# Stick-breaking attention heads: the logarithms of the key blocks behind summed on VectorE before the ones product

## What is computed

```python
z = einsum('bhqd,bhsd->bhqs', q_blk, kf) / sqrt(d)
past = key_pos[None, :] < q_pos[:, None]
log_not = where(past, log_sigmoid(-z), 0.0)
later = lax.cumsum(log_not, axis=3, reverse=True) - log_not
w = where(past, exp(log_sigmoid(z) + later), 0.0)
out = einsum('bhqs,bhsd->bhqd', w, vf)
```

## Time and profile before

| | |
|---|---|
| median of 3 executions | 2816.78 us (2816.77 to 2818.41) |
| profiled execution: its own time | 2817.07 us |
| its span | 2815.3 us |
| PE busy | 2766.5 us, 98% of the span |
| DVE busy | 1526.3 us, 54% |
| ACT busy | 1112.6 us, 40% |
| stick-breaking heads | about 1942 to 2335 us of the span |

### The profile page before, as it was taken

One profiled execution on the slowest core, in us unless ns is written; L12 is line 12 of the kernel. 1 busy time (PEld: TensorE's weight loads), 2 busy tenths in 40 slices (PEclk: granted clock), 3 DMA queues, 4 the chain that ended last, 5 costly groups with the idle time before them and its releaser, 6 DMA issues. The chain is left out here.

```text
span 2815.3 us, 33368 instructions
## 1 busy us (share of the span) xinstructions
PE 2766.5 (98%) x13174; PEld 2249.6 (80%) x13174; DVE 1526.3 (54%) x1830; ACT 1112.6 (40%) x1470; POOL 337.5 (12%) x409
## 2 busy tenths in 40 slices
PE   6999999999999999999999999899999999999999
PEld 2678888878888887888888888788878788788787
DVE  6867678774555546676743232534444434533643
ACT  7742222234344343343332332435555543432611
POOL 1011100000334223322311000100000000000000
PEclk8999999999999999999999999999999999999999
DMA  9647767654455554455455333232222223222252
GB/s 399 239 177 264 244 248 275 247 202 145 151 169 159 176 180 135 161 169 181 144 176 204 119 112 106 101 124 90 83 75 83 83 77 107 80 90 99 97 182 92
DMA packets 162122, 439.35 MB, mean 156 GB/s; under 512 B 14768, under 2 KB 59824, under 8 KB 151728
## 3 DMA queue, kind: packets, MB, share of 16 engines
q1 hardware_dynamic: 123360, 307.28, 32.1%
q0 software_dynamic: 15792, 92.99, 9.3%
q10 hardware_dynamic: 22816, 36.97, 3.7%
HBM read 398.11 MB, written 39.06 MB: 155 GB/s over the span
## 5 line engine op out<-in xcount | busy, mean ns | idle before, releaser
L1621 DVE TENSOR_TENSOR WL<-RAW,WH 128x1024 fp32r<-128x1024 f32 (+1 forms) x424 | 516.2, 1225 | 760.0 <-ACT WH L998 576.8
L408 PE MATMUL PB<-HH,WH 128*128 128x512 f32 x2048 | 817.5, 399 | 3.9 <-ACT zp L998 1.8
L413 PE MATMUL PB<-HL,WH 128*128 128x512 f32 x2048 | 802.0, 392 | 0.0
L414 PE MATMUL PB<-HH,WL 128*128 128x512 f32 x2048 | 801.5, 391 | 0.0
L998 ACT ACTIVATE WH<-RAW 128x1024 fp32r<-128x1024 f32 (+1 forms) x424 | 432.9, 1038 | 448.1 <-PE PB L521 259.1
L519 PE MATMUL PB<-WH,HH 128*128 128x512 f32 x1248 | 489.9, 393 | 0.8 <-DVE HL L1621 0.8
L521 PE MATMUL PB<-WH,HL 128*128 128x512 f32 x1248 | 486.1, 390 | 0.0
L520 PE MATMUL PB<-WL,HH 128*128 128x512 f32 x1248 | 485.9, 389 | 0.0
L408 PEld LDWEIGHTS PB<-HH,WH 128*128 128x128 f32 x2048 | 385.0, 188 | 92.0 <-issue 8.4
L414 PEld LDWEIGHTS PB<-HH,WL 128*128 128x128 f32 x2048 | 385.2, 188 | 66.7
L413 PEld LDWEIGHTS PB<-HL,WH 128*128 128x128 f32 x2048 | 385.7, 188 | 65.7 <-issue 3.1
(11 more groups left out here) (314 smaller groups left out, 2712.0 us busy)
## 6 DMA issues: line engine op xcount, KB each, us to landing
RAW<-in_w_in_t SPq DMA_DIRECT2D x320, 512.0 KB, 3.7
AU<-in_w_ada POOLq DMA_DIRECT2D x64, 1024.0 KB, 5.4
RAW<-in_w_out_t SPq DMA_DIRECT2D x96, 512.0 KB, 3.5
bcb<-R SPq DMA_DIRECT2D x64, 256.0 KB, 6.2
S<-so ACTq DMA_DIRECT2D x24, 384.0 KB, 2.4
ebc<-R SPq DMA_DIRECT2D x32, 256.0 KB, 6.3
SY<-evb ACTq DMA_DIRECT2D x32, 256.0 KB, 2.6
yin<-SY POOLq DMA_DIRECT2D x32, 256.0 KB, 4.2
```

What stands on the lines that cost most here:

```text
L408: h.matmul(banks[j], lh, m.HH[:, t, :], start=st, stop=False)
L413: h.matmul(banks[j], lh, m.HL[:, t, :], start=False, stop=False)
L414: ins = h.matmul(banks[j], ll, m.HH[:, t, :], start=False, stop=en)
L1621: return h.tensor_tensor(o, a, b, op)
```

## The change

The logarithms behind are first added up on VectorE, so that one product with `ones` serves for all the blocks behind. A new tile `LC` has 640 columns: 384 for key block 0 (the sum over blocks 1 to 3, for the queries of blocks 1, 2, 3), and 256 for block 1 (the sum over blocks 2 and 3). Block 2 has only block 3 behind it, and uses `LN` as it is. `LC` is split like `LN`, into `LCh` on ScalarE and `LCl` on VectorE. Blocks 1 and 3 now lie side by side in the tiles and share a bank of 512 columns, so three banks and 12 products do for a head. `LCh` and `LCl` lie where `COS` and `SIN` are later, so those two loads now wait for the last head.

```diff
-OFF = [0, 512, 896, 1152]
+OFF = [0, 512, 1024, 896]
+LATER = [(0, 512, (0,)), (512, 512, (1, 3)), (1024, 256, (2,))]
...
 # tensor_program, stick
             P.wait_ge(*at("LNl", hd))
+            P.wait_ge(*at("LCh", hd))
+            P.wait_ge(*at("LCl", hd))
             P.wait_ge(*at("exact"))
-            for sb in range(4):
-                b, bank = take(hb, "later", hd, sb)
-                for jb in range(sb, 4):
-                    for part in (m.LNh, m.LNl):
-                        ins = h.matmul(bank[:, (jb - sb) * 128:COLS[sb]], m.exact["triS" if jb == sb else "ones"],
-                                       part[:, OFF[jb]:OFF[jb] + COLS[jb]], start=jb == sb and part is m.LNh,
-                                       stop=jb == 3 and part is m.LNl)
+            for n, (o, w, blocks) in enumerate(LATER):
+                b, bank = take(hb, "later", hd, n)
+                for part in (m.LNh, m.LNl):
+                    h.matmul(bank[:, 0:w], m.exact["triS"], part[:, o:o + w], start=part is m.LNh, stop=False)
+                if n < 2:
+                    beyond = [x[:, (0, 384)[n]:(384, 640)[n]] for x in (m.LCh, m.LCl)]
+                else:
+                    beyond = [x[:, OFF[3]:OFF[3] + 128] for x in (m.LNh, m.LNl)]
+                to = bank[:, 128:COLS[n]]
+                h.matmul(to, m.exact["ones"], beyond[0], start=False, stop=False)
+                h.matmul(to, m.exact["ones"], beyond[1], start=False, stop=True).then_inc(*put(P.side, "later", hd, n))
 # scalar_program, stick
             A.then(act(m.LNh, m.LN, ACT.Copy), "LNh", hd)
             yield
-            yield
-            A.wait_ge(*at("logw", hd, 3))
+            A.wait_ge(*at("LC", hd))
+            A.then(act(m.LCh, m.LC, ACT.Copy), "LCh", hd)
+            yield
+            A.wait_ge(*at("logw", hd, 2))
 # vector_program
+    def later_blocks(hd):
+        LN, LC = m.LN, m.LC
+        V.then(h.tensor_copy(LC[:, 384:512], LN[:, OFF[2]:OFF[2] + 128]))
+        V.then(h.tensor_copy(LC[:, 0:128], LN[:, OFF[1]:OFF[1] + 128]))
+        t = V.then(TT(LC[:, 512:640], LN[:, OFF[2] + 128:OFF[2] + 256], LN[:, OFF[3]:OFF[3] + 128], ALU.add))
+        V.wait_ge(*t)
+        V.then(TT(LC[:, 128:384], LN[:, OFF[1] + 128:OFF[1] + 384], LC[:, 384:640], ALU.add), "LC", hd)
...
             yield
+            V.wait_ge(*at("ln masked", hd))
+            later_blocks(hd)
             V.wait_ge(*at("LNh", hd))
+            V.wait_ge(*at("LC", hd))
             V.then(TT(m.LNl, m.LN, m.LNh.bitcast(F32), ALU.subtract), "LNl", hd)
+            V.wait_ge(*at("LCh", hd))
+            V.then(TT(m.LCl, m.LC, m.LCh.bitcast(F32), ALU.subtract), "LCl", hd)
 # gpsimd_program, ahead of the loads of COS and SIN
+    G.wait_ge(*at("later", 7, 2))
```

More of the change, by code:

```diff
@@ L345, in memory @@
     m.COS, o = mem("COS", [128, 512], o)
+    m.LCh = at("LCh", o - 2 * KB, [128, 640], F32R)
     m.SIN, o = mem("SIN", [128, 512], o)
+    m.LCl = at("LCl", o, [128, 640], F32R)
+    m.LC, o = mem("LC", [128, 640], o)
     o = WA
@@ L877, in stick @@
             P.wait_ge(*at("LNl", hd))
+            P.wait_ge(*at("LCh", hd))
+            P.wait_ge(*at("LCl", hd))
             P.wait_ge(*at("exact"))
-            for sb in range(4):
-                b, bank = take(hb, "later", hd, sb)
-                for jb in range(sb, 4):
-                    for part in (m.LNh, m.LNl):
-                        ins = h.matmul(bank[:, (jb - sb) * 128:COLS[sb]], m.exact["triS" if jb == sb else "ones"],
-                                       part[:, OFF[jb]:OFF[jb] + COLS[jb]], start=jb == sb and part is m.LNh,
-                                       stop=jb == 3 and part is m.LNl)
-                ins.then_inc(*put(P.side, "later", hd, sb))
-                drop(hb, b, ("logw", hd, sb))
+            for n, (o, w, blocks) in enumerate(LATER):
[9 more added lines that the diff above has]
+                h.matmul(to, m.exact["ones"], beyond[1], start=False, stop=True).then_inc(*put(P.side, "later", hd, n))
+                drop(hb, b, ("logw", hd, n))
             yield
@@ L1419, in e_free @@
             A.wait_ge(*at("av", 2 * p - 1))
-            A.wait_ge(*at("later", 2 * p - 1, 3))
+            A.wait_ge(*at("later", 2 * p - 1, 2))
         else:
@@ L1477, in stick @@
             if hd:
-                A.wait_ge(*at("later", hd - 1, 3))
+                A.wait_ge(*at("later", hd - 1, 2))
             A.then(act(m.LNh, m.LN, ACT.Copy), "LNh", hd)
             yield
+            A.wait_ge(*at("LC", hd))
+            A.then(act(m.LCh, m.LC, ACT.Copy), "LCh", hd)
             yield
-            A.wait_ge(*at("logw", hd, 3))
+            A.wait_ge(*at("logw", hd, 2))
             A.then(act(m.E1, m.E1, ACT.Exp), "w exp2", hd)
@@ L2162, in stick @@
             if hd:
-                V.wait_ge(*at("later", hd - 1, 3))
+                V.wait_ge(*at("later", hd - 1, 2))
             for sb in range(4):
@@ L2171, in stick @@
             yield
+            V.wait_ge(*at("ln masked", hd))
+            later_blocks(hd)
             V.wait_ge(*at("LNh", hd))
+            V.wait_ge(*at("LC", hd))
             V.then(TT(m.LNl, m.LN, m.LNh.bitcast(F32), ALU.subtract), "LNl", hd)
+            V.wait_ge(*at("LCh", hd))
+            V.then(TT(m.LCl, m.LC, m.LCh.bitcast(F32), ALU.subtract), "LCl", hd)
             yield
[L2175 to L2180, removed]
+            for n, (o, w, blocks) in enumerate(LATER):
+                for sb in blocks:
+                    V.wait_ge(*at("beta", hd, sb))
+                V.wait_ge(*at("later", hd, n))
+                V.then(TT(m.E1[:, o:o + w], m.E1[:, o:o + w], bank("later", hd, n)[:, 0:w], ALU.subtract),
+                       "logw", hd, n)
             yield
```

## The result

The median went from 2816.78 us to 2823.95 us (9 executions each; 2815.12 to 2818.41 before, 2820.99 to 2827.02 after); the ratio is 1.0025, with a 95% interval of 1.0016 to 1.0033, so some 4.5 to 9.3 us slower. The profiled execution took 2823.95 us, its span is 2822.2.

A forecast was written before the change was run, and what follows sets the result against it. TensorE was taken as the bound, busy 398.47 of 400 us in the heads. Waits less savings, +4.9 us, plus 4.2 for the clock gave +9.1: 2826.2 for the profiled execution, 2825.9 as median (+0.32%); range 2819.5 to 2829.0.

The forecast's parts named there:

- Products: TensorE's running-sum block in each head: 2.72 us falls to 1.96, saving 0.76 a head, 6.1 us in eight.
- `LC` and `LCh`: Odd heads: VectorE takes 1.08 us for LC, each copy 0.19; ScalarE waits some 2.4 us for it before LCh.
- The chain: Heads 1, 3, 5: roots 3.1 us late, normalisation through masks moved by 2.95, av 2.9 later; TensorE waits 3.7 us.
- The 0.15: Handover of 0.15 us from the masks' end to av on TensorE, so heads 1 and 5 have no slack.
- Five heads without loss: Head 7 and the even heads keep their 0.76 us, 3.8 in all; head 7 tightest for LCl, 0.5 us left.
- Loads of `COS` and `SIN`: Loads after the last head: land by about 2332, first use at 2337.1, so nothing waits.
- The sum without the clock: Whole program: three odd heads lose 2.9 us each, less 3.8 us gained in the other five: +4.9 us.
- The clock: Granted clock falls to 0.50 behind each odd-head wait on TensorE, costing 1.4 us each, 4.2 us for three.
- Rival 1: The wait before av comes, but the clock doesn't fall, or once: 2821.7 us, or 2823.1 with one fall; chance 0.20.
- Rival 2: Odd heads' chain doesn't move, so TensorE's shorter blocks count in full: 2810.7 us, -0.22%; chance 0.09.
- Rival 3: Chain moves by less, one head is spared, or another TensorE wait shrinks: 2813 to 2820 us; chance 0.12.
- Rival 4: COS and SIN late, holding VectorE: time up to a few us more; chance 0.01.

The follow-up runs named there:

- experiment 2: Changed kernel with LC, LCh and LCl made but unused, and the 20 products and four banks of before: 2828.69 us against 2816.17, ratio 1.0045.
- experiment 3: Changed kernel, but LCh written by VectorE right behind LC, not by ScalarE: 2814.28 us against 2816.17 for the kernel before, ratio 0.9993.
- experiment 5: Changed kernel, but VectorE makes LC as soon as the head's logarithms are masked; LCh stays on ScalarE: 2812.32 us against 2815.67 before, ratio 0.9985.
- experiment 6: Changed kernel with LC made early and LCh on VectorE: 2811.30 us against 2815.67 for the kernel before, ratio 0.9982.
- experiment 7: Changed kernel with LC early, LCh on VectorE, odd heads' masks ahead of VectorE's next weight unit: 2807.83 us against 2815.67 before, ratio 0.9970.
- experiment 8: Kernel before, with only the odd heads' masks moved ahead of VectorE's next weight unit: 2814.72 us against 2815.67, ratio 0.9997.
- experiment 9: Changed kernel unaltered, a second profiled execution, for the clock: 2822.68 us against 2815.93 for the kernel before.
- experiment 10: Changed kernel unaltered, a third profiled execution, for the clock: 2822.41 us against 2815.93 for the kernel before.
- experiment 1: Changed kernel with its 12 products but no LC, LCh or LCl, products reading LNh and LNl: 2811.91 us against 2816.17 before, ratio 0.9986.
- experiment 4: Changed kernel, but in odd heads VectorE masks the weights ahead of its next weight unit: 2813.90 us against 2816.17 before, ratio 0.9994.

## Why the prediction was right, and where it was off

**Direction, mechanism and size.** 2825.9 was forecast, +9.1 us; measured +7.2 (4.5 to 9.3), inside the range. Each step of the working can be found in the profile:

- *Products.* 1.96 us a block forecast, 1.94 measured (2008.81 to 2010.75 in head 1; 2.00 in heads 2 and 6); 0.78 saved, not 0.76. The estimate by the Trainium skill's spacings, 0.65, was the poorer one (TensorE: Matmul & The Clock Gate, Back-to-back issue gap).
- *`LC` and `LCh`.* Two copies take less of VectorE than I took: 0.22 us each in their rows, and the next begins after 0.13 to 0.14. The wait of ScalarE was 2.28 us (2.4 forecast).
- *The chain.* Counted from the start of head 1's products (2012.72 before, 2008.81 after), the first `SHs` came 3.0 us later (3.1 forecast; -3.58 after, -6.61 before), the normalisation 2.8 (2.95), `av` 2.67 (2.9). Between the last two lie the `logw` saved (0.07) and the handover: `av` starts 0.05 us behind the end of the masks (2018.82 + 0.89 to 2019.76), where it had been 0.15. The 0.15 was read rightly and is there in experiment 2 too, with the 20 products; in every kernel with the 12 products that waits there it is 0.05. Why is open. The wait of 3.34 us in the row is a delay of 3.49 (10.95 less 7.46), against the 3.7 forecast.
- *Five heads without loss.* So it was: 3.9 us gained, 3.8 forecast. That `LCl` was nearest to being late in head 7 was wrong: the prediction looked at heads 0 and 7 alone. In the changed kernel `LCl` ends 0.47 us ahead of the products in head 7, but 0.15 in heads 2 and 6, whose blocks took 2.00 us, not 1.94; experiment 3 then made these two wait.
- *Loads of `COS` and `SIN`.* No wait for them shows: `COS` is issued at 2335.1, lands 3.0 us later and is first read at 2344.0. (The prediction's own figures add up to 2330.3 for the landing, not 2332; nothing hangs on it.)
- *The sum without the clock.* +4.9 forecast; 7.6 - 3.9 = +3.7 measured. Heads 1 and 3 lost 2.67 each, not 2.9, and head 5 lost 2.30: before, it took 8.65 us and not 8.28, so 0.37 us of its delay was there already. The prediction had that wait in its rows and didn't take it off.
- *The clock.* 4.2 us forecast as 1.4 each time. It varies from execution to execution: 6.2, 1.6 and 2.9 us in three, 3.6 on average. The medians agree: +7.2 less 3.7 leaves 3.5. So the term was 0.6 too large on average, and wrong in kind: not 1.4 each, but nothing or 1.7 to 2.9. That it came so near is luck, in two ways. It stood on a single fall, behind a wait after which the clock fell in six of twelve executions; and two errors offset each other, since five of nine waits were followed by a fall and not all, while a fall cost 2.1 us on average and not 1.4. Nor does it begin at a fixed delay of 2.9 us from the wait's start: in the first execution the clock fell 3.5, 4.0 and 2.2 us behind it. Whether it widens the spread of the times isn't shown: that was 6.0 us in nine executions against 3.3 before, but 28 executions of the kernel before on the chip of experiments 5 to 8 spread over 8.7.

**The rivals.** Rival 1, no fall of the clock or one, is what experiments 9 and 10 show, with one fall each; its time with one fall, 2823.1, is 0.9 us from the measured median, the forecast 2.0. What was right is what the two have in common, the direction and the waits. Rival 2, faster with all eight heads gaining, was out because of the order on ScalarE and VectorE alone: experiment 7 gives it back with the same arithmetic in another order, `LCh` on VectorE. Rival 3, a chain that moves by less in one of the heads, is out: all three moved, and the wait of 1.08 us at 2108.67 is still there, 1.09 us. Rival 4 is out by the loads above.

**What is shown and what is argued.** Shown: the loss is all in the side work (1 and 2), in its place rather than its amount (5 and 6 against the changed kernel), and goes through the chain that ends in the masks (4 and 7). The link between the wait and the clock is shown by its place in the profiles and by its absence behind these heads' waits of 1.2 us and less (experiments 1 and 3 to 6). Why it falls after one wait of 3.3 us and not after another stays open.

## What to carry to other kernels

An operation given to a half idle engine can cost time through what stands behind it in that engine's program order until the next thing that the busy engine waits for; look for the place, not the busy share. Where work has to go in, put it where the engine was idle anyway (here VectorE's 1.1 us ahead of its weight unit), make the sums as early as their inputs allow, and let no other engine stand waiting for them. Look through all the places of one kind: the tightest heads were two that hadn't been looked at. When the bound engine gets faster, the chains that were just in time become the bound, so shorten them in the same change: the products alone were worth 4.3 us, the version with the masks moved too 7.8.

## What the runs showed of the hardware

- A wait of 2.7 us or 3.3 us on TensorE was followed by the 0.50 clock in 2 of 3 (experiment 2) and 5 of 9 cases (the changed kernel three times), the one of 1.8 us near 170 us in 6 of 12. One of 0.5 to 1.2 us before `av` never was (15 cases, experiments 1 and 3 to 6), nor was the one of 1.1 us near 2108 us, in all 12 profiled executions.
- A cast of 128x640 to the rounded format of the high parts (fp32r in the rows) takes 0.49 us on VectorE, where a subtraction of that width takes 0.82, and a copy to it on ScalarE 0.74. The instructions of the tile `LCh` in experiment 3 (ns min/median/max, first and last start, shapes):

```profile
L2194 DVE CAST LCh<-LC x8: 493/494/496, 1959.4 to 2318.6; 128x640 fp32r<-128x640 f32 x8
L1631 DVE TENSOR_TENSOR LCl<-LC,LCh x8: 817/818/820, 1961.2 to 2320.4; 128x640 fp32r<-128x640 f32 x8
```
